# Two-layer transformer kernel: attention heads and retention heads in pairs, one turn of TensorE in every fourth unit

## The reference

```python
# first layer, per head
s = where(k_pos <= q_pos, (q @ k.T) * scale, -inf);  attn = softmax(s) @ v
# second layer, per attention head: one softmax over summed windows
y_a = dilated_attention_mixture(q_a, k_a, v_a) * silu(z_a)
# second layer, per retention head
o = ((q @ k.T) * decay) @ v;  y_r = o * rsqrt(mean(o * o) + eps) * silu(z_r)
```

## Time and profile before

| | |
|---|---|
| median of 3 runs | 1535.81 us (1535.54 to 1535.85) |
| the profiled execution | 1534.71 us |
| its span on the core | 1533.0 us, 32039 instructions |
| PE, DVE, ACT busy | 99%, 74%, 51% of the span |
| granted TensorE clock, mean | 0.997 |
| chain that ended last | PE 94%, DVE 4%, ACT 1% |

### The profile page before, as it was taken

The page is one execution under the profiler, slowest core; times in us unless marked ns, Lnnn a source line. Parts: engine busy times, 40 slices in busy tenths (PEclk is TensorE's granted clock), DMA queues, the critical chain, the costliest instruction groups (busy, mean ns, idle before and its releaser), DMA issues.

```text
span 1533.0 us, 32039 instructions
## 1 busy us (share of the span) xinstructions
PE 1520.6 (99%) x12566; PEld 1480.7 (97%) x12566; DVE 1134.8 (74%) x1371; ACT 778.1 (51%) x930; POOL 35.4 (2%) x64
## 2 busy tenths in 40 slices
PE   9999999999999999999999999999999999999997
PEld 8999998999999999999999999999999989999997
DVE  7877777658988878878788887879854644764754
ACT  7645456545554445444444444445554643454544
POOL 0000001000000000000000000000000000000000
PEclk9999999999999999999999999999999999999998
DMA  9574566457876867767677776866475554455451
GB/s 351 168 272 159 203 191 246 155 173 265 311 291 239 299 222 274 260 237 285 238 272 240 260 272 223 297 228 210 147 251 194 193 192 165 154 162 179 164 180 56
DMA packets 86412, 340.31 MB, mean 222 GB/s; under 512 B 9896, under 2 KB 10424, under 8 KB 79808
## 3 DMA queue, kind: packets, MB, share of 16 engines
q1 hardware_dynamic: 77760, 281.05, 52.9%
q0 software_dynamic: 7712, 55.63, 10.2%
q10 hardware_dynamic: 864, 2.53, 0.4%
HBM read 337.03 MB, written 2.14 MB: 221 GB/s over the span
## 4 chain that ended last, share of the span: by engine, by line
PE 94%; DVE 4%; ACT 1%; issue 1%; DMA 0%; SPq 0%; DVEq 0%; ACTq 0%
PE PS L1328 27%; PE PS L1330 27%; PE PS L1332 27%; PE PS L1377 3%; PE PS L1376 3%; PE PS L1374 3%; DVE wlo L696 1%; PE PS L1523 1%; PE PS L1544 1%; ACT whi L333 1%; DVE conv_acc L777 1%; DMA raw<-weights 0%; PE PS L1701 0%; PE PS L1506 0%; DVE EM L881 0%
## 5 line engine op out<-in xcount | busy, mean ns | idle before, releaser
L696 DVE TENSOR_TENSOR wlo<-raw,whi 128x1024 fp32r<-128x1024 f32 x528 | 642.8, 1222 | 337.0 <-ACT whi L333 333.6
L333 ACT ACTIVATE whi<-raw 128x1024 fp32r<-128x1024 f32 x528 | 557.4, 1059 | 640.2 <-PE PS L1332 571.0
L1328 PE MATMUL PS<-gh,whi 128*128 128x256 f32 x3096 | 863.4, 279 | 0.7 <-DVE wlo L696 0.4
L1330 PE MATMUL PS<-gl,whi 128*128 128x256 f32 x3096 | 856.1, 277 | 0.0
L1332 PE MATMUL PS<-gh,wlo 128*128 128x256 f32 x3096 | 856.1, 277 | 0.0
L1328 PEld LDWEIGHTS PS<-gh,whi 128*128 128x128 f32 x3096 | 581.7, 188 | 5.6 <-issue 2.4
L1330 PEld LDWEIGHTS PS<-gl,whi 128*128 128x128 f32 x3096 | 581.4, 188 | 0.8
L1332 PEld LDWEIGHTS PS<-gh,wlo 128*128 128x128 f32 x3096 | 581.6, 188 | 0.0
L1328 PE MATMUL PS<-ah,whi 128*128 128x256 f32 x688 | 189.9, 276 | 0.0
L1330 PE MATMUL PS<-al,whi 128*128 128x256 f32 x688 | 189.9, 276 | 0.0
L1332 PE MATMUL PS<-ah,wlo 128*128 128x256 f32 x688 | 189.9, 276 | 0.0
(11 more groups left out here) (254 smaller groups left out, 892.9 us busy)
## 6 DMA issues: line engine op xcount, KB each, us to landing
raw<-weights SPq DMA_DIRECT2D x528, 512.0 KB, 3.5
ada_w<-w_ada POOLq DMA_DIRECT2D x48, 1024.0 KB, 6.5
EM<-rows POOLq DMA_DIRECT2D x1, 3072.0 KB, 12.4
X<-xT SPq DMA_DIRECT2D x3, 512.0 KB, 8.2
c<-const ACTq DMA_DIRECT2D x1, 1536.0 KB, 6.9
c_act<-c_rows POOLq DMA_DIRECT2D x1, 1024.0 KB, 6.7
KF<-factors POOLq DMA_DIRECT2D x2, 512.0 KB, 6.6
outT<-X SPq DMA_DIRECT2D x2, 512.0 KB, 3.2
```

The costliest lines, as they stand in the source:

```text
L333: act.activation(whi[:, j % SPLIT, :], raw[:, j, :], ACT.Copy).then_inc(s_hi, 1)
L696: dve.tensor_tensor(wlo[:, j % SPLIT, :], raw[:, j, :], whi[:, j % SPLIT, :].bitcast(F32), ALU.subtract).then_inc(s_lo, 1)
L1328: pe.matmul(out[:, t, :], whi[:, b, w], hi[:, kt, :], start=first and half == 0 and (apart or t % 2 == 0), stop=False, skip_group_check=True)
L1330: pe.matmul(out[:, t, :], whi[:, b, w], lo[:, kt, :], start=False, stop=False, skip_group_check=True)
```

## The change

Heads go in pairs. In attention a pair starts every fourth slot (78, 82, 86, 90 in the first layer, 84, 88 and 108, 112 in the second). PE runs step 0 of both heads in the pair's slot 0, the transposes of both in slot 4, the values of both in slot 8, where those of a head came two slots after its transposes. DVE and ACT go by the tables `DVE_STEPS` and `ACT_STEPS` (slot within the pair, odd head, step): DVE takes the scores of the even head in slot 0, those of the odd head and the normalising of the even one in slot 1, the normalising of the odd head in slot 2. In retention the pairs start at slots 64 and 68, and PE's three steps come in slots 0, 4 and 8. The order of PE within a first-layer turn: transposes of both heads, then scores of each new head alternating with values of an old one.

So that two heads fit at a time, scores, transposes and results move to other places in banks 4 to 7 (`score_part`, `turned_part`, `value_bank`, `retained_bank`), and waits on the head before become waits on the pair before. Some are new: in the first layer DVE waits for the scores of both heads before it reads those of either, DVE's second part of an odd head waits for ACT's copy of an older head (`s_pts`), ACT's copy for an odd head waits for the scores of the next pair (`s_sc`), and in the second layer the values wait until DVE has read scores that share the bank (`s_sb`). No matmul is added or left out; the two idle matmuls stay where they are. The diff, with unchanged lines cut; the hunks left out change bank and step numbers of retention on ACT and DVE in the same way:

```diff
@@ -184,6 +184,34 @@
         TURNS = (3, 5, 7, 9, 11, 13, 15)
+        ACT_STEPS = ((1, 0, 1), (2, 1, 1), (4, 0, 4), (4, 1, 4), (8, 0, 6), (8, 1, 6))
+        DVE_STEPS = ((0, 0, 0), (1, 1, 0), (1, 0, 1), (2, 1, 1), (8, 0, 6), (8, 1, 6))
+        def score_part(h, layer, c):
+            odd = h % 2
+            if layer:
+                return PS[:, 7 if odd else 4, S * c:S * c + S]
+            if odd:
+                return PS[:, 5, 0:S] if c else PS[:, 4, 3 * P:4 * P]
+            return PS[:, 4, P:3 * P] if c else PS[:, 4, 0:P]
+        def turned_part(h, layer, b):
+            odd = h % 2
+            if layer:
+                return PS[:, 5 + odd, S * b:S * b + S]
+            if odd:
+                return PS[:, 7, 3 * P:4 * P] if b else PS[:, 5, S:2 * S]
+            return PS[:, 7, S:3 * P] if b else PS[:, 7, 0:S]
+        def value_bank(h, layer):
+            return PS[:, 4 if layer else 6, S * (h % 2):S * (h % 2) + S]
+        def retained_bank(r):
+            return PS[:, 6 + r % 2, :]
@@ -440,31 +468,36 @@
                 if step == 4:
-                    act.wait_ge(s_pt, H + 1)
+                    act.wait_ge(s_pt, H + 2 - h % 2)
                     if H >= 2:
...
                     if layer:
-                        act.activation(PTS[:, h % 2, :, :], PS[:, 5, :].rearrange("p (c d) -> p c d", c=2),
+                        act.activation(PTS[:, h % 2, :, :], PS[:, 5 + h % 2, :].rearrange("p (c d) -> p c d", c=2),
+                                       ACT.Copy).then_inc(s_pts, 1)
+                    elif h % 2 == 0:
+                        act.activation(PTS[:, 0, :, :].rearrange("p c d -> p (c d)")[:, 0:3 * P], PS[:, 7, 0:3 * P],
                                        ACT.Copy).then_inc(s_pts, 1)
                     else:
-                        act.activation(PTS[:, h % 2, :, :].rearrange("p c d -> p (c d)")[:, 0:3 * P], PS[:, 5, 0:3 * P],
-                                       ACT.Copy).then_inc(s_pts, 1)
+                        act.activation(PTS[:, 1, 1, 0:P], turned_part(h, 0, 1), ACT.Copy)
+                        if h + 2 < HEADS:
+                            act.wait_ge(s_sc, H + 3)
+                        act.activation(PTS[:, 1, 0, :], turned_part(h, 0, 0), ACT.Copy).then_inc(s_pts, 1)
                 if step == 6 and layer == 0:
-                    act.wait_ge(s_pv, H + 1)
+                    act.wait_ge(s_pv, H + 2 - h % 2)
                     if h < 4:
-                        act.activation(QKVZ[:, Q0 + h, :], PS[:, 6, 0:S], ACT.Copy).then_inc(s_ahi, 1)
+                        act.activation(QKVZ[:, Q0 + h, :], value_bank(h, 0), ACT.Copy).then_inc(s_ahi, 1)
                     else:
-                        act.activation(gh[:, 8 + h, :], PS[:, 6, 0:S], ACT.Copy).then_inc(s_ahi, 1)
+                        act.activation(gh[:, 8 + h, :], value_bank(h, 0), ACT.Copy).then_inc(s_ahi, 1)
                 if step == 6 and layer == 1 and h >= 4:
...
-                for h in reversed(range(h0, h0 + heads)):
-                    step = n - (b + 2 * (h - h0))
-                    if 0 <= step < 7:
-                        attention(step, h, layer)
+                for pair in reversed(range(heads // 2)):
+                    for at, odd, step in ACT_STEPS:
+                        if n - (b + 4 * pair) == at:
+                            attention(step, h0 + 2 * pair + odd, layer)
@@ -923,12 +956,13 @@
                                                       c2[:, 1, :, :], ALU.mult, ALU.add))
-                    dve.wait_ge(s_sc, H + 1)
+                    dve.wait_ge(s_sc, H + 1 if layer else H + 2 - h % 2)
                     if H >= 2:
...
                     if layer:
-                        dve.scalar_tensor_tensor(SB[:, h % 2, :, :], PS[:, 4, :].rearrange("p (c d) -> p c d", c=2),
+                        dve.scalar_tensor_tensor(SB[:, h % 2, :, :],
+                                                 PS[:, 7 if h % 2 else 4, :].rearrange("p (c d) -> p c d", c=2),
                                                  SCALE, SB[:, h % 2, :, :], ALU.mult, ALU.add).then_inc(s_sb, 1)
@@ -936,7 +970,9 @@
                         for c, at in enumerate((slice(0, P), slice(P, 3 * P))):
-                            ins = dve.scalar_tensor_tensor(seen(h, c), PS[:, 4, at], q_col(h, c), mask[:, at],
+                            if c and h % 2 and h >= 2:
+                                dve.wait_ge(s_pts, h - 1)
+                            ins = dve.scalar_tensor_tensor(seen(h, c), score_part(h, 0, c), q_col(h, c), mask[:, at],
                                                            ALU.mult, ALU.add)
@@ -950,23 +986,24 @@
                 if step == 6 and layer:
-                    dve.wait_ge(s_pv, H + 1)
+                    dve.wait_ge(s_pv, H + 2 - h % 2)
                     z = QB[:, ZA2 + h, :]
-                    dve.tensor_tensor(z, PS[:, 6, 0:S], z, ALU.mult).then_inc(s_gated, 1)
+                    dve.tensor_tensor(z, value_bank(h, 1), z, ALU.mult).then_inc(s_gated, 1)
                     if h >= 4:
...
                 if step == 6 and not layer and h >= 4:
-                    dve.wait_ge(s_ahi, h + 1)
-                    dve.tensor_tensor(gl[:, 8 + h, :], PS[:, 6, 0:S], gh[:, 8 + h, :].bitcast(F32),
+                    dve.wait_ge(s_ahi, h + 2 - h % 2)
+                    dve.tensor_tensor(gl[:, 8 + h, :], value_bank(h, 0), gh[:, 8 + h, :].bitcast(F32),
                                       ALU.subtract).then_inc(s_gl, 1)
...
             def attention_slot(n, b, h0, heads, layer):
-                for h in reversed(range(h0, h0 + heads)):
-                    step = n - (b + 2 * (h - h0))
-                    if 0 <= step < 7:
-                        attention(step, h, layer)
+                for pair in reversed(range(heads // 2)):
+                    for at, odd, step in DVE_STEPS:
+                        if n - (b + 4 * pair) == at:
+                            attention(step, h0 + 2 * pair + odd, layer)
@@ -1492,20 +1529,18 @@
                 if step == 4:
-                    if layer:
-                        pe.wait_ge(s_rrt, RET_HEADS)
-                    else:
+                    if not layer:
                         pe.wait_ge(s_qk, HEADS)
                     pe.wait_ge(s_pn, 2 * H + 2)
-                    if H >= 1:
-                        pe.wait_ge(s_pts, H)
+                    if h >= 2:
+                        pe.wait_ge(s_pts, H - h % 2)
                     for c in range(2):
...
                             src = SB[:, h % 2, c, P * b:P * b + P] if layer else seen(h, c)[:, P * b:P * b + P]
-                            at = S * b + (P * c if layer or not b else 0)
-                            mm = pe.transpose(PS[:, 5, at:at + P], src, ident)
+                            at = P * c if layer or not b else 0
+                            mm = pe.transpose(turned_part(h, layer, b)[:, at:at + P], src, ident)
                     mm.then_inc(s_pt, 1)
-                if step == 6:
+                if step == 8:
                     weighted(h, layer, PTS, v, (1, 0))
@@ -1515,12 +1550,16 @@
                             pe.wait_ge(s_evac, (G_IN2 + 10 if h < 4 else G_IN2 + 13) + 2)
+                            if h == 0:
+                                pe.wait_ge(s_rrt, RET_HEADS)
+                            if h == 4:
+                                pe.wait_ge(s_gated, 4)
                         else:
                             pe.wait_ge(s_qk, h + 1)
-                        if H >= 1:
-                            pe.wait_ge(s_sb, H)
-                    at, keys = (S * c, S) if layer else (P * c, P + P * c)
-                    mm = pe.matmul(PS[:, 4, at:at + keys], q[:, P * c:P * c + P], k[:, 0:keys], start=True, stop=True)
+                        if H >= 2:
+                            pe.wait_ge(s_sb, H - h % 2)
+                    keys = S if layer else P + P * c
+                    mm = pe.matmul(score_part(h, layer, c), q[:, P * c:P * c + P], k[:, 0:keys], start=True, stop=True)
                     if c == 1:
@@ -1534,38 +1573,43 @@
                             pe.wait_ge(s_evac, (G_IN + 10 if h < 4 else G_OUT) + 2)
-                        if layer and h:
-                            pe.wait_ge(s_gated, h)
-                        if not layer and h:
+                        if layer and h % 2 == 0:
+                            pe.wait_ge(s_sb, HEADS + h // 4 * 4 + 3)
+                            if h:
+                                pe.wait_ge(s_gated, h)
+                        if not layer and h and h % 2 == 0:
                             pe.wait_ge(s_ahi, h)
...
                     first = 0 if layer else P * b
-                    mm = pe.matmul(PS[:, 6, first:S], v(b, P * (h % 4)), PTS[:, h % 2, b, 0:S - first],
+                    mm = pe.matmul(value_bank(h, layer)[:, first:S], v(b, P * (h % 4)), PTS[:, h % 2, b, 0:S - first],
```

(84 more changed lines are left out.)

2 lines of the change are left out of this document (removed).

## The result

| | before | after |
|---|---|---|
| median | 1535.54 us | 1541.13 us |
| ratio | | 1.0037, 95% interval 1.0027 to 1.0047 |
| span of the profiled execution | 1533.0 us | 1539.1 us |

A forecast was written before the change was run, and what follows sets the result against it. PE was taken as the bound, busy 1520.6 of 1533.0 us. Terms -0.3, +1.3, +0.15 and 0 sum to +1.2 us: 1535.9 profiled, 1537.0 as median (56%), range 1534.4 to 1539.9.

The forecast's parts named there:

- Boundaries, -0.3: PE's turns (small matmuls between stream units) fall from 32 to 18; 14 boundaries at 0.02 us save 0.3, bounds 0 and 0.4.
- rival of 0.19 a boundary: Each boundary is worth the long interval after a turn, 0.19 us: 2.7 us less, 1534.5 with the wait; 12%.
- Turn 82, +1.3: First layer, after unit 82: PE's transposes wait for DVE's key tiles and head 1's normalising, 1.3 us lost, bounds 0 and 1.8.
- Turn 76, +0.15: Retention, after unit 76: PE waits for DVE's work on heads 2 and 3, 0.15 us, bounds 0 and 0.5.
- Turns 86, 90 and the second layer: Later first-layer attention turns and second-layer heads: DVE is in time, so no wait of PE.
- Two pitches, 0: PE's stream runs at 0.1135 or 0.1177 us per matmul; change in slow units taken as 0, bounds -1.6 and +3.2.
- the slow pitch spreads: Rival: more stream units turn slow, 0.10 us each; from 19 more the time is over 1538.9 us; 13%.
- bound of +3.2: Upper bound of the pitch term in us: all 46 narrow units in the stretches of the change slow.
- 1.2 forecast: Sum of boundaries, the waits at turns 82 and 76 and the pitch: +1.2 us over the kernel before.

The follow-up runs named there:

- only_ret: Only the retention heads go in pairs, against the kernel before, with attention in both layers as before: 1535.67 us, 1.0000 (0.9990 to 1.0010).
- idle_after_last: The changed kernel with two idle fp32 matmuls of 256 columns added after unit 121 of the second layer: 1539.95 us, 1.0027 (1.0017 to 1.0038).

## Why the prediction was wrong, step by step

- **Boundaries, -0.3:** right. 0.02 each from only_ret, and the four-matmul turn of the changed kernel has nothing left over beside its matmuls. The rival of 0.19 a boundary falls. The Trainium skill ("TensorE: Matmul & The Clock Gate", "Single matmul latency") gives some 166 ns that a single warm matmul takes beside its columns. Charged to each turn, as the prediction tried it, that doesn't fit either: the runs here show 0.02 us.
- **Turn 82, +1.3:** right in place, cause and size: 1.40, where I had the key tiles at 0.3 (0.38) and head 1 near 259.85 (260.29, in an execution that was 0.28 later before the change could act). The walk through DVE's queue, each step from start to start, was worth its length.
- **Turn 76, +0.15:** nothing to be seen; inside its bounds. Turns 86, 90 and the second layer: no wait, as forecast.
- **Two pitches, 0:** this step failed. The price of a slow unit (0.10) was right, and the rival "the slow pitch spreads" is what happened: 36 units more, worth 3.8 us, where 19 were its threshold. I gave it 13% and took zero as the middle for reasons that don't hold. First, I wrote that pure 256-column turns of two matmuls leave the stream quick and stand before the long stretches; that is so for the idle turn after slot 99, but the last turn of each half of the second layer grew from two such matmuls to four by this change, and behind them lie 7 and 23 narrow units. Second, I counted only the units between turns (46), not these 30, so the bound of +3.2 was too small as well. Third, "All the pure 256-column turns of two matmuls leave it quick" and "only a turn or a stall switches between them" were not so in the kernel before either: turns 84 and 86 are such turns, unit 87 of 512 columns behind them settles at the quick pitch of its width, and unit 88 runs at 0.1178 from its first matmuls on, with no turn between; units 111 and 112 do the same. Without the 30 units the sum would still have been 0.9 short: of the 5.2 us in the stretches of the change, 30 x 0.104 are 3.1, and 2.1 are left for the 1.2 forecast. Those 0.9 are six more slow units of 256 columns (0.6) and five of 512 (0.3). (The kernel has six groups of 512-column units, not four; nothing rests on that.)

What would have found it: list every turn of the change with its count of instructions and the length of stream behind it, and refuse to call a pitch unknown and therefore zero where a long stream hangs on one turn.

## What to carry to other kernels

Fewer switches between a stream and small work are worth what a switch costs beside its matmuls, and that is read by putting turns of one, two and six matmuls on a line; here it was 0.02 us, so grouping had at most 0.3 us to win. Grouping moves the small work's inputs to an earlier deadline: walk the helper engine's queue in its new order before it is grouped. And a busy engine can still lose time in its pitch: compare starts over a whole unit, in every stretch behind a changed point, since no table of waits shows it.

## What the runs showed of the hardware

The stream of fp32r matmuls of 256 columns has two stable pitches, 0.1133 and 0.1177 us, at a granted clock of 1.00 in both, and keeps one for long: units 128 to 375 of the feed-forward are quick throughout. A short stall can be enough to switch it. At unit 376, without a turn, the distance behind the first matmul is 0.14 to 0.15 us in every trace; behind it the next eight units are slow in 4 of the 13 traces and quick in 9, with the same code. Units 91 to 94 of the first layer, too, were slow in one execution (idle_after_last) and quick in another (the changed kernel) with the same code there.

Idle turns of 4, 8, 12 and 16 matmuls, and of 4, 8 and 16 transposes, left it slow in all 10 cases, and counts not divisible by four left it quick in all 16. These are readings from two executions, in one stream of 256 columns. Real turns don't obey the count. The retention turn of seven before left the stream slow, the idle turn of seven quick. In the changed kernel turns 88 and 112 (four matmuls and eight transposes) left it slow, and turns 92 and 116, of four matmuls and eight transposes as well, turned a slow stream quick, though the profile shows no wait in any of them. Turn 108, four matmuls, turned a slow stream of 512 columns quick (0.233 to 0.229). So a count of four explains the two long stretches behind turns 96 and 120 and the idle turns, and is no rule for every turn. Why the count matters there, and whether the order in a turn or instructions that carry a wait count with it, stays open. So do the 0.4 us of the feed-forward: its time differs by up to 0.55 between executions of unchanged code without a slow unit in them.
